# Order of logarithms, exponentials and reductions in the RMS norms of a diffusion backbone step, on one core

## What is computed

```python
def rmsnorm(x, g):
    xf = x.astype(F32)
    y = xf * lax.rsqrt(jnp.mean(xf * xf, axis=-1, keepdims=True) + EPS)
    return (y * g.astype(F32)).astype(x.dtype)

def modulate(h, shift, scale):
    return h * (1 + scale) + shift

for l in range(DEPTH):
    hs = modulate(rmsnorm(xs, norm1_g[l]), m_lat[0], m_lat[1])
    ...                       # attention and pooling, or gated linear attention
    xs = xs + m_lat[2] * out_s
    hs = modulate(rmsnorm(xs, norm2_g[l]), m_lat[3], m_lat[4])
    xs = xs + m_lat[5] * swiglu(hs, w_ffn_in[l], w_ffn_out[l])
y_sample = rmsnorm(xs, final_g)
```

## Time and profile before

| | |
|---|---|
| median of 3 runs | 3305.63 us (3289.94 to 3310.71) |
| profiled execution | 3302.27 us, span 3300.4 us |
| mean granted TensorE clock | 0.926 |
| busy: PE, DVE, ACT, POOL | 2940.1, 1424.4, 828.6, 756.6 us |
| instructions: PE, DVE, ACT, POOL | 16762, 3065, 1086, 273 |

### The profile page before, as it was taken

One profiled execution on the slowest core, in us unless ns is written; L12 is line 12 of the kernel. 1 busy time (PEld: TensorE's weight loads), 2 busy tenths in 40 slices (PEclk: granted clock), 3 DMA queues, 4 the chain that ended last, 5 costly groups with the idle time before them and its releaser, 6 DMA issues. The chain is left out here.

```text
span 3300.4 us, 42789 instructions
## 1 busy us (share of the span) xinstructions
PE 2940.1 (89%) x16762; PEld 2826.2 (86%) x16762; DVE 1424.4 (43%) x3065; ACT 828.6 (25%) x1086; POOL 756.6 (23%) x273
## 2 busy tenths in 40 slices
PE   5897688769999999999499969996969999999995
PEld 5897577769999999999399957776969999999994
DVE  4687787582322232233444345553452232222225
ACT  3300567143111111110500034442061111111113
POOL 1553122233121111220412112221151212111210
PEclk9999899889999999999799977765989999999997
DMA  5234100422111111100334312103111111111101
GB/s 216 77 114 130 27 14 1 171 77 77 39 38 51 38 38 38 47 29 0 118 128 144 126 74 75 57 34 116 58 77 39 38 51 51 38 38 38 50 1 57
DMA packets 56951, 217.14 MB, mean 66 GB/s; under 512 B 7024, under 2 KB 20016, under 8 KB 47536
## 3 DMA queue, kind: packets, MB, share of 16 engines
q1 hardware_dynamic: 54288, 207.80, 18.1%
q10 hardware_dynamic: 2592, 8.38, 0.6%
HBM read 186.80 MB, written 25.17 MB: 64 GB/s over the span
## 5 line engine op out<-in xcount | busy, mean ns | idle before, releaser
L544 PE MATMUL ps<-hh,wi_hi 128*128 128x384 f32 x2112 | 709.2, 336 | 9.1 <-POOL hl L414 5.8
L545 PE MATMUL ps<-hl,wi_hi 128*128 128x384 f32 x2112 | 708.3, 335 | 0.0
L546 PE MATMUL ps<-hh,wi_lo 128*128 128x384 f32 x2112 | 707.9, 335 | 0.0
L926 DVE TENSOR_TENSOR hid<-ps,hid 128x384 f32<-128x384 f32 x132 | 73.4, 558 | 1047.0 <-ACT hid L836 1017.8
L544 PE MATMUL ps<-hh,whi 128*128 128x384 f32 x1152 | 390.6, 339 | 46.3 <-POOL wlo L657 29.8
L544 PEld LDWEIGHTS ps<-hh,wi_hi 128*128 128x128 f32 x2112 | 398.6, 189 | 12.6 <-POOL hl L414 6.4
L545 PEld LDWEIGHTS ps<-hl,wi_hi 128*128 128x128 f32 x2112 | 398.8, 189 | 0.0
L546 PEld LDWEIGHTS ps<-hh,wi_lo 128*128 128x128 f32 x2112 | 398.7, 189 | 0.0
L546 PE MATMUL ps<-hh,wlo 128*128 128x384 f32 x1152 | 389.0, 338 | 0.0
L545 PE MATMUL ps<-hl,whi 128*128 128x384 f32 x1152 | 388.9, 338 | 0.0
L916 DVE SCALAR_TENSOR_TENSOR x<-ps,mod,x 128x128 f32<-128x128 f32 (+1 forms) x704 | 327.2, 512 | 77.7 <-PE ps L546 73.0
(11 more groups left out here) (201 smaller groups left out, 4001.6 us busy)
## 6 DMA issues: line engine op xcount, KB each, us to landing
raw_in<-in_w_ffn_in_dram SPq DMA_DIRECT2D x44, 1024.0 KB, 4.8
wmt<-in_w_mod_t_dram SPq DMA_DIRECT2D x80, 512.0 KB, 3.5
raw_out<-in_w_ffn_out_dram SPq DMA_DIRECT2D x22, 1024.0 KB, 4.8
gla_spill<-turn SPq DMA_DIRECT2D x24, 576.0 KB, 3.0
head<-gla_spill SPq DMA_DIRECT2D x12, 1152.0 KB, 6.2
raw<-in_w_in_odd_dram SPq DMA_DIRECT2D x24, 512.0 KB, 3.6
raw<-in_w_in_even_dram SPq DMA_DIRECT2D x16, 512.0 KB, 5.1
wm<-in_w_mod_dram SPq DMA_DIRECT2D x12, 512.0 KB, 9.1
```

The source lines that it names most:

```text
L544: pe.matmul(acc, w_hi, in_hi, start=first, stop=False)
L545: pe.matmul(acc, w_hi, in_lo, start=False, stop=False)
L546: return pe.matmul(acc, w_lo, in_hi, start=False, stop=last)
L926: dve.tensor_tensor(hid[:, t], ps[:, 2 * t + 1, 0:CW], hid[:, t], ALU.mult).then_inc(hid_done, 1)
```

## The change

In `act_late` the logarithms of all three thirds now stand ahead of the three exponentials, and both ahead of the first Identity. In `vector` all three sums stand ahead of the first scaling. Nothing is computed differently, and no semaphore, tile or transfer is changed.

```diff
-            def root(c):
+            for c in range(NC):
                 act.wait_ge(self.averaged, c + 1)
                 act.activation(self.stat[:, c], self.bank[c], ACT.Ln, bias=eps[:], scale=1.0 / D).then_inc(self.logged, 1)
+            for c in range(NC):
                 act.wait_ge(self.logged, c + 1)
                 act.activation(self.stat[:, c], self.stat[:, c], ACT.Exp, scale=-0.5).then_inc(self.rooted, 1)
-            root(0)
             for c in range(NC):
-                if c + 1 < NC:
-                    root(c + 1)
                 for h in range(2):
                     act.wait_ge(self.scaled, 2 * c + h + 1)
...
-            total(0)
             for c in range(NC):
-                if c + 1 < NC:
-                    total(c + 1)
+                total(c)
+            for c in range(NC):
                 dve.wait_ge(self.rooted, c + 1)
```

## The result

| | before | changed |
|---|---|---|
| median, 17 runs each | 3304.57 us (3284.28 to 3310.71) | 3318.18 us (3311.74 to 3323.26) |
| profiled execution's span | 3300.4 us | 3316.7 us |
| mean granted TensorE clock | 0.926 | 0.923 |
| busy: PE, DVE, ACT, POOL | 2940.1, 1424.4, 828.6, 756.6 us | 2939.9, 1422.3, 802.3, 756.1 us |

The ratio is 1.0059, with a 95% interval from 1.0043 to 1.0074: slower, by less than 1%.

A forecast was written before the change was run, and what follows sets the result against it. ScalarE's stream was taken to set each norm's end, with TensorE busy 89% of the span. The norms' 3.5 + 3.8 - 3.1 + 3.8 + 3.7 = +11.7 us on 3302.3 gave 3314.0, range 3299 to 3325.

The forecast's parts named there:

- First Identity: First norm, ScalarE: the first Identity starts at 83.3 instead of 76.17, 7.1 us late.
- Shorter stream: First norm, ScalarE: the 3.6 us of Ln, Exp and two loads inside the stream go; net +3.5 us at the last subtraction.
- GpSimd: First norm: six scalings in one piece hold the first subtraction, late by about 10, until 91.8; last subtraction +3.5 us.
- The FFNs' norms: Norms ahead of the two FFNs: last subtraction +3.4 us, third 1 on TensorE +3.8 us each, between +3.3 and +6.0.
- VectorE's condition: FFN: VectorE makes hid for third 1 only when all subtractions are done; +3.4 us, low bound +3.3.
- TensorE's condition: FFN: TensorE must finish third 0, fed later and partly at half clock, at 762.6; third 1 starts at 762.7 to 763.2.
- rival (c): Clock stays low longer after longer idle time: FFNs +6.0 us each, projections a few, +17 to +22 in all; 12 in 100.
- Layer 1's norm: Norm of layer 1: third reduction fits in VectorE's idle time; first Identity +0.5, minus 3.6, so -3.1 us.
- Final norm: Last norm: 7.1 us late, 3.6 shorter, plus 0.2 for stores closer together, so +3.7 us.
- (a): All norms: the loads pay, first Identity not late, only the break goes; 18 us faster, 3284; 5 in 100.
- (b): TensorE follows the first delivery of third 0, delay undiminished in four norms; about +40 us, 3342; 3 in 100.
- (d): Stages behind the norms have slack that swallows the delay; nothing measurable, 3302 to 3306 us; 12 in 100.

The follow-up runs named there:

- the three comparisons: The unchanged kernel before and the changed kernel measured against each other three times: changed medians 3318.18, 3316.46 and 3315.90 us, ratios 1.0059, 1.0046 and 1.0029.
- the kernel with VectorE's part alone: Against the kernel before: all three sums ahead of the first scaling, ScalarE's order and all its loads as before; 3318.56 us, ratio 1.0043.
- the kernel with all six loads ahead: VectorE as changed; ScalarE does Ln, Exp three times, each with its table load, ahead of the first Identity; 3309.3 us, ratio to before 1.0011.
- The break put back: Against the changed kernel: a one-column Ln and Exp, each with a table load, added behind third 0's second Copy; 3325.51 us, ratio to before 1.0071.
- the kernel with the square root: Against the kernel before, order kept: ScalarE takes Sqrt instead of Ln and Exp, VectorE a reciprocal; 3309.97 us, ratio 1.0010.

## Why the prediction was right

It said 3314.0 us in a range of 3299 to 3325, from a sum of +11.7 us. The medians of the three comparisons are 3316 to 3318, and the parts came out one by one, but for two details that did not matter to the total:

- **First Identity.** Forecast 7.1 us late, measured 24.8 - 17.7 = 7.1. The step that carried it, "VectorE's third reduction now starts where the scaling started", is seen in the row of three reductions in 16.03 us, and the kernel with VectorE's part alone shows that this move makes 2.9 of the 7.1 us. The other 4.2 come from ScalarE's order, as the kernel with all six loads ahead confirms in part: there the first exponential does not wait for the third logarithm, and the first Identity is 1.9 us sooner with four loads more.
- **Shorter stream.** Forecast -3.6, end of the first norm +3.5; measured +3.4. The break put back showed that a microsecond of break is a microsecond at the end.
- **GpSimd.** Here a detail was wrong, without effect. "All six scalings run in one piece and the first subtraction waits until 91.8, ends at 95.2": it ended at 93.08. It was asked for at 88.35, 0.32 us after VectorE's fifth scaling had begun, and went in ahead of the sixth; VectorE's six took 13.34 instead of 10.1. The first subtraction began 7.1 us later than before, counted from the first square, and not the 10 that the prediction gave as a sign. In the earlier trace rows the subtraction asked 0.7 us after a scaling had begun and the next scaling went first; in the kernel with the square root it asked 0.73 us after one had begun and went ahead of the next. Who goes first is not settled here. The end of the norm did not depend on it, as the step said: the last subtraction waited 0.43 us for ScalarE. The Trainium skill's rule on the shared port pair ("SBUF — State Buffer", "SBUF: two separate sides") agrees with these rows, a scaling and a subtraction never ran together.
- **The FFNs' norms.** Last subtraction forecast +3.4, measured +3.3. Third 1's start in the first FFN, on TensorE and VectorE (against the earlier trace rows):

```profile
773.34 0.56 DVE L923 TENSOR_TENSOR hid<-ps,hid 128x384 f32<-128x384 f32 x1 [17.87 <-POOL hl L411]
...
773.95 0.44 PE L541 MATMUL ps<-hh,wi_hi 128*128 128x384 f32 x1 [0.25 <-DVE hid L923]
```

  From the first square that is 55.0 us against 51.7, +3.3, the lower bound: VectorE's condition alone. In the second FFN TensorE's condition decided, +4.7 (3.3 at the norm and 1.4 behind it). The cause is the clock, shown by the granted clock in the first four microseconds of third 0's second half, in the first and the second FFN of the changed kernel:

```profile
758.90:762.90 4.00, 4.00 (x23) 4.00 (x24) 0.00 (x0) 3.97 (x6) 4.00 (x2) 1.00 0.00 0
...
2446.60:2450.60 4.00, 4.00 (x13) 4.00 (x14) 0.00 (x0) 3.97 (x6) 4.00 (x2) 0.50 0.00 0
```

  In the first the clock was back when the second half began, in the second it stayed at half for 13 more matmuls. This is rival (c), in one FFN and with 1.4 us. Taken together the two FFNs cost 8.0 us against 2 x 3.8, but neither cost 3.8: that the sum fits is in part luck. The kernel with VectorE's part alone pays 1.3 there by the other way shown above, a wait so long that the clock is down for third 1. The kernel before does the same in the first FFN in two of three profiles (811.8 us behind the norm instead of 810.3), so only the second FFN, with 808.9 in all three profiles of before and 810.1 to 810.3 in all four of the changed kernel, tells the two apart.
- **Layer 1's norm.** Forecast -3.1, measured -3.2. Against the earlier trace rows, ScalarE, and the third matmul, which waits for the first logarithm:

```profile
1601.24 1.28 ACT L366 ACT_TABLE_LOAD   x1
...
1604.91 0.58 ACT L366 ACTIVATE stat<-ps,eps 128x384 f32<-128x384 f32 x1 [1.33 <-PE ps L405]
...
1609.15 3.61 ACT L380 ACTIVATE hl_f<-hl_f,mod,amod 128x128 f32<-128x128 f32 x8 [1.00 <-DVE hl_f L396]
...
1603.26 1.62 PE L405 MATMUL ps<-stat,ones 128*128 128x384 f32 x2 [4.55 <-ACT stat L366]
```

  The first Identity starts 7.9 us after the first load, against 7.35 before; "+0.5" held, and the kernel changed in this norm alone gained as much.
- **Final norm.** Forecast +3.7, measured +3.8: ScalarE's last work ends 3.4 later, and the stores now follow without a gap (against the earlier trace rows; slices of 0.775 us from 3286 on):

```profile
3295.96 13.73 ACT L378 ACTIVATE hl_f<-hl_f,gnorm 128x128 f32<-128x128 f32 x32 [1.00 <-DVE hl_f L396]
...
GB/s 0 0 0 0 0 0 0 0 0 0 0 0 0 0 0 0 0 0 0 0 0 46 379 375 369 369 325 385 371 365 381 363 339 371 373 377 363 379 165 0
```

- **The rivals.** (a), the loads pay, fell: 30, 10 and 30 loads stand in kernels of 12.7, 12.0 and 6.1 us loss, and 5 in the one with the square root, which was no faster than before. The figure of the Trainium skill's "ScalarE: Activation LUTs", section "What ACT_TABLE_LOAD costs", for a drain on top of the load is not borne out: from the end of Ln at 79.48 to the start of Exp at 80.80 lie 1.32 us, the load of 1.28 included. (b), the first delivery, fell: TensorE got the first half 5.9 us later in the first norm, and the norm's end moved 3.4. (d), slack that swallows the delay, is not seen: the stretches behind the norms are as long as before within their scatter.

The forecast was made against the profiled execution before, 3302.3 us. The changed kernel's took 3318.5, 4.5 us over the forecast, and this is the 8.1 us by which the stretch from the first norm to the FFN was longer that time, less 3.5 in the one behind layer 1's norm; the other three profiles of the changed kernel had spans of 3311.1, 3316.8 and 3316.1.

## What to carry to other kernels

A table load costs its 1.28 us only where its engine is what the others wait for. Ask of each load whether the engine would have waited there anyway, and of each batching what the first consumer now waits for: here three thirds had to be summed before the first could be scaled, and 7 us at the head of a stream outweighed 3.6 saved in its middle, though 20 loads were gone. The same edit gained in the one norm whose first third was held up by something else, so decide it place by place; and when a version wins or loses a few microseconds in a kernel that scatters by ten, cut the stretch out of the profile and compare that.

## What the runs showed of the hardware

- A reciprocal of 128x384 in float32 on VectorE took 2.54 us, where 128x1 took 0.16.
- A waiting subtraction on GpSimd got in between two scalings that stood back to back on VectorE in two cases (asked 0.32 us into the fifth of six in the changed kernel, 0.73 us into the first of two in the one with the square root) and not in another (0.7 us into the first of two, before).
- A reciprocal was not held up like this: one took its usual 2.54 us (92.39 to 94.93) while a subtraction ran (to 95.79).
- The granted clock came back at different times after the same pattern of work: in the two FFNs of the changed kernel the windows above show 1.00 and 0.50 at the same place of the stage. A stage that gets its clock back sooner need not end sooner: the kernel with VectorE's part alone had 1.00 in its second half, waited 5.11 us and began the next third at 0.64.
